# First three outputs behind five layer norms: un-normed sums, corrected afterwards

## The reference

```
def layer_norm(x, g, b):
    mu = mean(x); xc = x - mu; var = mean(xc * xc)
    return xc * rsqrt(var + 1e-5) * g + b

for layer in (0, 1):
    x = layer_norm(ALPHA * x + 0.5 * ff(x, ...), g[layer, 0], b[layer, 0])
    mix = rglru_block(x) if layer == 0 else dilated_attention(x, k, v)
    x = layer_norm(ALPHA * x + mix, g[layer, 1], b[layer, 1])
    x = layer_norm(ALPHA * x + 0.5 * ff(x, ...), g[layer, 2], b[layer, 2])
    if layer == 0: k, v = x @ kv_w
```

## Time and profile before

| | us |
|---|---|
| median of three runs | 1878.16 |
| lowest, highest | 1875.6, 1890.77 |
| span of the profiled execution | 1878.1 |
| PE busy in it | 1823.2 (97%) |
| DVE, ACT, POOL busy | 1263.5, 1160.7, 408.0 |

### The profile page before, as it was taken

How to read it: one execution, slowest core, us unless ns; L and a number is a source line. 1 busy time by engine, 2 the same in 40 slices (tenths; PEclk the granted TensorE clock), 3 DMA queues, 4 the chain that set the end, 5 groups by cost and what they waited for, 6 DMA issues and landing times.

```text
span 1878.1 us, 32925 instructions
## 1 busy us (share of the span) xinstructions
PE 1823.2 (97%) x11312; PEld 1606.1 (86%) x11312; DVE 1263.5 (67%) x1912; ACT 1160.7 (62%) x1894; POOL 408.0 (22%) x442
## 2 busy tenths in 40 slices
PE   7999999999899999999999999999999999999998
PEld 6879888898688888888898988889888888778887
DVE  5877676774766857666668867666566566666665
ACT  4465574643555746488638868844588454759863
POOL 1103330230441402011122032212021120541212
PEclk9999999999899999999999999999999999999999
DMA  6515356557433555555643546663555636126562
GB/s 232 174 57 179 102 194 187 185 184 197 133 107 111 191 188 185 186 186 185 215 162 135 181 134 202 202 209 116 196 184 197 204 128 207 51 79 201 186 222 74
DMA packets 86764, 312.11 MB, mean 166 GB/s; under 512 B 10368, under 2 KB 15616, under 8 KB 86400
## 3 DMA queue, kind: packets, MB, share of 16 engines
q1 hardware_dynamic: 86368, 309.01, 50.6%
q10 hardware_dynamic: 288, 1.64, 0.3%
HBM read 309.56 MB, written 1.05 MB: 165 GB/s over the span
## 4 chain that ended last, share of the span: by engine, by line
PE 89%; DVE 6%; ACT 2%; issue 2%; POOL 1%; DMA 0%; POOLq 0%; SPq 0%; ACTq 0%; DVEq 0%
PE pt L505 42%; PE pt L506 21%; PE pt L499 5%; PE pt L500 5%; PE pt L501 5%; DVE w_lo L1852 1%; PE pt L619 1%; PE pt L623 1%; PE pt L621 1%; PE pt L1149 1%; PE pt L934 1%; DVE in_both L1880 1%; ACT w_hi L1260 1%; PE pt L636 0%; PE pt L1052 0%
## 5 line engine op out<-in xcount | busy, mean ns | idle before, releaser
L1852 DVE TENSOR_TENSOR w_lo<-raw,w_hi 128x1024 fp32r<-128x1024 f32 (+2 forms) x548 | 706.0, 1289 | 290.6 <-ACT w_hi L1260 282.6
L1260 ACT ACTIVATE w_hi<-raw 128x1024 fp32r<-128x1024 f32 (+2 forms) x548 | 598.7, 1095 | 403.6 <-PE pt L506 227.4
L505 PE MATMUL pt<-in_both,w_hi 128*128 128x512 f32 x2103 | 740.4, 397 | 0.5 <-DVE in_both L2434 0.5
L506 PE MATMUL pt<-in_both,w_lo 128*128 128x256 f32 x2103 | 588.5, 280 | 0.0
L505 PEld LDWEIGHTS pt<-in_both,w_hi 128*128 128x128 f32 x2103 | 395.4, 188 | 97.0 <-DVE w_lo L1852 1.1
L505 PE MATMUL pt<-act_both,w_hi 128*128 128x512 f32 x1309 | 463.0, 398 | 0.0
L506 PEld LDWEIGHTS pt<-in_both,w_lo 128*128 128x128 f32 x2103 | 397.2, 189 | 0.1
L506 PE MATMUL pt<-act_both,w_lo 128*128 128x256 f32 x1309 | 366.3, 280 | 0.0
L505 PEld LDWEIGHTS pt<-act_both,w_hi 128*128 128x128 f32 x1309 | 245.7, 188 | 60.5 <-issue 1.7
L506 PEld LDWEIGHTS pt<-act_both,w_lo 128*128 128x128 f32 x1309 | 246.9, 189 | 0.2
L2606 POOL TENSOR_TENSOR act_both<-scr,act_both 128x256 f32 x88 | 99.8, 1134 | 494.7 <-ACT act_both L1739 494.7
(11 more groups left out here) (328 smaller groups left out, 2308.3 us busy)
## 6 DMA issues: line engine op xcount, KB each, us to landing
raw<-in_fi SPq DMA_DIRECT2D x176, 512.0 KB, 3.6
raw<-in_ff SPq DMA_DIRECT2D x128, 512.0 KB, 3.5
raw<-in_fo SPq DMA_DIRECT2D x64, 704.0 KB, 4.1
raw<-in_dq SPq DMA_DIRECT2D x24, 512.0 KB, 3.7
raw<-in_mq SPq DMA_DIRECT2D x16, 512.0 KB, 3.7
raw<-in_mo SPq DMA_DIRECT2D x16, 512.0 KB, 4.0
raw<-in_rg_u SPq DMA_DIRECT2D x10, 512.0 KB, 3.4
raw<-in_rg_y SPq DMA_DIRECT2D x10, 512.0 KB, 3.6
```

The source lines that it names most:

```text
L505: nc.tensor.matmul(pt[:, b, :], lhs_hi, both.rearrange("p t s -> p (t s)"), start=start, stop=False)
L506: return nc.tensor.matmul(pt[:, b, 0:S], lhs_lo, both[:, 0, :], start=False, stop=stop)
L1260: nc.scalar.activation(w_hi[:, u.slot(), w], raw[:, u.slot(), w], ACT.Copy).then_inc(hi_split, 1)
L1852: v.tensor_tensor(w_lo[:, u.slot(), w], raw[:, u.slot(), w], w_hi[:, u.slot(), w].bitcast(F32), ALU.subtract).then_inc(lo_split, 1)
```

## The change

At norms 0 to 4 the first three outputs of the next projection no longer wait for the normed input. With g and b the gain and bias, m the rest of the mean and r the inverse root, W(g * (y - m) * r + b) = (W(g*y) - m * Wg) * r + Wb. So ACT and DVE write z = g*y in high and low parts over parts of act_both that are free (`z_high`, `z_low`), with g and b as two more columns (258 in all), and PE makes the three outputs from z (`from_normed_sums`). Between its second and third chunk PE also makes the sums of the norm, now with a square matrix of ones and 256 columns, so that mean and variance stand on all partitions; root and inverse are taken on 128 x 256. DVE then corrects the three outputs (`z_columns`, `z_open`, `z_scale`). All other outputs use the normed input as before, the fourth being the first that waits for it. For each stage behind a norm the corrected outputs get steps of their own (`first_outputs` for swiglu, `first_conv0` and a convolution from SBUF for rg, linked blocks for kv_k and dq). POOL takes off the mean from all eight chunks instead of five. Norm 5 is as before (`last_norm`).

The diff, cut to its core:

```diff
+Z_WIDE = 3
...
+            def from_normed_sums(name, n):
+                z = z_both(n)
+                pe.wait_ge(acc_free, LN_ACC[n] + DC - 1)
+                for k in range(DC):
+                    pe.wait_ge(z_ready, DC * n + k + 1)
+                    w = slice(k * P, k * P + P)
+                    for j in range(Z_WIDE):
+                        u = UNIT0[name] + j
+                        if k == 0:
+                            pe.wait_ge(lo_split, u + 1)
+                        o = pt[:, j, 0:S + 2]
+                        mm = three(o, w_hi[:, u % RING, w], w_lo[:, u % RING, w], z[:, k, 0, :], z[:, k, 1, :],
+                                   k == 0, k == DC - 1)
+                        if k == DC - 1:
+                            mm.then_inc(unit_used, 1)
+                    if k == 1:
+                        pe.wait_ge(rest_part, 3 * n + 3)
+                        nc.tensor.matmul(pt[:, 6, 0:S], ones, rest_sum, start=True, stop=True).then_inc(rest_ready, 1)
+                        pe.wait_ge(sq_sum, 6 * (n + 1))
+                        nc.tensor.matmul(pt[:, 4, 0:S], ones, spare[:, 0, :], start=True, stop=False)
+                        pe.wait_ge(lnsq_ready, DC * (n + 1))
+                        nc.tensor.matmul(pt[:, 4, 0:S], ones, spare[:, DC - 1, :], start=False, stop=True
+                                         ).then_inc(var_ready, 1)
...
-                if upm == 1 and wait_src:
+                if normed is not None:
+                    from_normed_sums(name, normed)
+                    done = Z_WIDE
...
-                                if k + j == 0 and wait_src:
+                                if k + j == (0 if normed is None else Z_WIDE) and wait_src:
...
+                        if n == Z_WIDE:
+                            pe.wait_ge(in_ready, IN0["ln0"] + k + 1)
...
+                    if m.base == DC - 1 and n in (0, 2, 3):
+                        z_gains_hi(n)
+                        for k in range(DC - 1):
+                            z_high(n, k)
                     if m.base > FIRST_MEAN:
                         act.wait_ge(acc_free, LN_ACC[n] + m.base + 1)
                         square(m.base)
+                    if m.base == FIRST_MEAN + 1 and n in (1, 4):
+                        z_gains_hi(n)
+                        for k in range(FIRST_MEAN + 2):
+                            z_high(n, k)
+                    if m.base == DC - 2 and n in (1, 4):
+                        z_high(n, DC - 2)
...
+            def z_gains_hi(n):
+                act.wait_ge(unit_used, LN_LAST[n] if n in (0, 2, 3) else LN_LAST[n] - DC + 2)
+                nc.scalar.activation(z_both(n)[:, :, 0, S:S + 2], z_gains(n), ACT.Copy).then_inc(z_gains_high, 1)
+            def z_high(n, k):
+                nc.scalar.activation(z_both(n)[:, k, 0, 0:S], y[:, k, :], ACT.Copy, scale=gain("lng", n * DC + k)
+                                     ).then_inc(z_hi_ready, 1)
+            def shift(n, out, k):
+                return nc.scalar.activation(out[:, k, :], y[:, k, :], ACT.Identity, bias=gain("lnb", n * DC + k))
+            def layer_norm(n):
+                split(Pos(LN_LAST[n] + RING))
+                z_high(n, DC - 1)
+                act.wait_ge(rest_ready, n + 1)
+                nc.scalar.activation(spread_wide, pt[:, 6, 0:S], ACT.Square, scale=1.0 / D).then_inc(rest_squared, 1)
+                nc.scalar.activation(mean_wide, pt[:, 6, 0:S], ACT.Copy, scale=1.0 / D).then_inc(rest_copied, 1)
+                act.wait_ge(var_done, n + 1)
+                nc.scalar.activation(spread_wide, spread_wide, ACT.Sqrt, bias=lneps).then_inc(ln_root, 1)
+                for k in range(DC):
+                    act.wait_ge(ln_scaled, DC * n + k + 1)
+                    shift(n, in_hi, k).then_inc(in_hi_ready, 1)
+                for k in range(DC):
+                    shift(n, x, k).then_inc(ln_out, 1)
...
+                def first_outputs():
+                    u0 = UNIT0[f"fi{l}{f}"]
+                    s0 = Z_SCALED0[f"fi{l}{f}"]
+                    split(Pos(u0 + RING))
+                    act.wait_ge(z_scaled, s0 + 1)
+                    nc.scalar.activation(act_a[0], act_b[0], ACT.Silu, bias=z_cols[:, 1:2]).then_inc(silu_ready, 1)
+                    split(Pos(u0 + 1 + RING))
+                    act.wait_ge(unit_used, u0 + Z_WIDE)
+                    after(Pos(1))
+                    split(Pos(u0 + 2 + RING))
+                    act.wait_ge(z_scaled, s0 + 2)
+                    nc.scalar.activation(act_a[1], act_b[1], ACT.Silu, bias=z_cols[:, 5:6]).then_inc(silu_ready, 1)
+                    act.wait_ge(unit_used, u0 + 4)
+                    half(Pos(3))
+                    split(Pos(u0 + 3 + RING))
+                    after(Pos(3))
+                if n in (2, 5):
+                    first_outputs()
+                    units(f"fi{l}{f}", before=half, after=after, begun=4)
+                else:
...
+            def first_conv0(j):
+                act.wait_ge(z_scaled, j + 1)
+                nc.scalar.activation(z_first[j], z_first[j], ACT.Identity, bias=z_cols[:, 2 * j + 1:2 * j + 2]
+                                     ).then_inc(u_made, 1)
+                act.wait_ge(u_made, j + 1)
+                nc.scalar.activation(big[:, j, :], z_first[j], ACT.Identity, bias=gain("cb", j),
+                                     scale=gain("cw", 3 * RC + j)).then_inc(conv0, 1)
+            for j in range(Z_WIDE):
+                split(Pos(UNIT0["rg"] + j + RING))
+                first_conv0(j)
+                if j == 0:
+                    act.wait_ge(unit_used, UNIT0["rg"] + Z_WIDE)
+                else:
+                    conv_hi(j - 1)
+            nc.scalar.activation(warm, eps, ACT.Tanh)
             for n, (kind, i) in enumerate(RG_ORDER):
...
+            def z_low(n, k):
+                dve.wait_ge(z_hi_ready, DC * n + k + 1)
+                z = z_both(n)
+                v.scalar_tensor_tensor(out=z[:, k, 1, 0:S], in0=y[:, k, :], scalar=gain("lng", n * DC + k),
+                                       in1=z[:, k, 0, 0:S].bitcast(F32), op0=ALU.mult, op1=ALU.subtract
+                                       ).then_inc(z_ready, 1)
+            def z_ahead(n):
+                def go():
+                    dve.wait_ge(z_gains_high, n + 1)
+                    z = z_both(n)
+                    v.tensor_tensor(z[:, :, 1, S:S + 2], z_gains(n), z[:, :, 0, S:S + 2].bitcast(F32), ALU.subtract)
+                    for k in range(3):
+                        z_low(n, k)
+                return go
+            def scaled(n, k):
+                dve.wait_ge(recentred, DC * n + k + 1)
+                v.scalar_tensor_tensor(out=y[:, k, :], in0=y[:, k, :], scalar=gain("lng", n * DC + k),
+                                       in1=rstd_all, op0=ALU.mult, op1=ALU.mult).then_inc(ln_scaled, 1)
+            def layer_norm(n):
+                for k in range(3, DC - 1):
+                    z_low(n, k)
+                split(Pos(LN_LAST[n] + RING))
+                z_low(n, DC - 1)
+                dve.wait_ge(var_ready, n + 1)
+                dve.wait_ge(rest_squared, n + 1)
+                v.scalar_tensor_tensor(out=spread_wide, in0=pt[:, 4, 0:S], scalar=1.0 / D, in1=spread_wide,
+                                       op0=ALU.mult, op1=ALU.subtract).then_inc(var_done, 1)
+                dve.wait_ge(ln_root, n + 1)
+                v.reciprocal(rstd_all, spread_wide).then_inc(ln_inverse, 1)
+                dve.wait_ge(ln_inverse, n + 1)
+                for k in range(DC + 2):
+                    if k < DC:
+                        scaled(n, k)
+                    if k >= 2:
+                        dve.wait_ge(in_hi_ready, IN0[f"ln{n}"] + k - 1)
+                        v.scalar_tensor_tensor(out=in_lo[:, k - 2, :], in0=y[:, k - 2, :],
+                                               scalar=gain("lnb", n * DC + k - 2), in1=in_hi[:, k - 2, :].bitcast(F32),
+                                               op0=ALU.add, op1=ALU.subtract).then_inc(in_ready, 1)
+            def z_columns(name):
+                dve.wait_ge(unit_used, UNIT0[name] + Z_WIDE)
+                link(v.tensor_copy(z_cols.rearrange("p (j t) -> p j t", t=2), pt[:, 0:Z_WIDE, S:S + 2]))
+            def z_open(name, j, dest):
+                v.scalar_tensor_tensor(out=dest, in0=mean_wide, scalar=z_cols[:, 2 * j:2 * j + 1], in1=pt[:, j, 0:S],
+                                       op0=ALU.mult, op1=ALU.subtract).then_inc(acc_free, 1)
+            def z_scale(name, j, dest, factor):
+                dve.wait_ge(acc_free, ACC0[name] + j + 1)
+                return v.scalar_tensor_tensor(out=dest, in0=dest, scalar=-factor, in1=rstd_all,
+                                              op0=ALU.mult, op1=ALU.mult)
...
+                def first_outputs():
+                    u0 = UNIT0[name]
+                    z_columns(name)
+                    z_open(name, 0, act_b[0])
```

(48 more changed lines are left out.)

205 lines of the change are left out of this document (108 added, 97 removed).

## The result

The changed kernel takes **1904.86 us** (median of four runs, 1900.63 to 1905.85) against 1880.6 us for the kernel before on the same chip (four runs): ratio 1.0114, 95% interval 1.0091 to 1.0138. It is 1.1% slower. The profiled execution has a span of 1904.0 us, 25.9 us more than the earlier trace rows.

The account below looks back on a forecast made before the run. PE was taken as the bound, holding 89% of the chain. 1878.1 us, plus 10.3 for lags at five norms, 2.5 for one clock fall and 1 for DVE beside POOL, gave 1892 us; range 1867 to 1904.

Parts of the forecast that it names:

- The likeliest case: Whole kernel: the prediction's own forecast, 1892 us, 0.7% slower, within 1884 to 1897; chance 0.50.
- DVE beside POOL: At each norm, DVE work slowed beside POOL: 0.2 us per norm, 1 us in all.
- the clock: PE's granted clock falling around output five: 0 to 8 us together, one fall of 2.5 us taken.
- The wait at the norm goes: PE at norm 1: 5.6 us lost before; now three outputs end at +9.8 rather than +14.1.
- The x writes stand ahead of the fifth split, and output five comes later than before: ACT at norm 1: x writes end at +16.05, then the split; PE idles 4.4 us, starting output five at +18.35, before +17.1.
- The chain to output five: Norm 1: reciprocal from +4.9, last low part of the normed input at +13.45, output five at +18.35.
- The rival in which DVE and POOL take turns: Scalings beside POOL's subtractions: 3 us per norm, 13 in place of 1 in all, 1904 us; chance 0.08.
- That rival (0.15): Granted clock falls at every norm: 8 us in place of 2.5, 1897.5 us; chance 0.15.
- Norm 0: Recurrent block (rg), where ACT and DVE set the pace: conv(3) at +27.9, second gate at +32.9, lag +5.1 us.
- Norms 1, 2, 4: Lags of +2.65, -0.7 and +2.9 us, from late weight splits and steps on ACT and DVE.
- Norm 3: Query projection (dq): output eight ends at +30.3, before +30.0, a lag of +0.3 us.
- Nothing is given back behind output eight: Stages behind the norms: lags stay whole; said at norm 0, where nothing behind has less to do.

## Where the prediction was right and where it was wrong, point by point

The likeliest case, 1892 us, was 12.9 us too low, and the time lies 0.9 us above the upper end of 1904. Part of that is the base: the forecast started from 1878.1 us, and the kernel before took 1880.6 beside the changed one. Taken as a slowdown, 13.9 us were forecast and 24.3 measured, a ratio of 1.007 against 1.011, and the upper end of the range, 1.014, holds. The direction and the mechanism were right, the size was too small: two terms of the sum, DVE beside POOL and the clock, were mis-sized. The chance of "slower by over 1%" was put at 0.20; with an interval of 0.9 to 1.4% the result does not quite decide that.

*The wait at the norm goes.* Right: matmuls of 258 columns follow the last output at once at four norms, 0.69 us late at norm 4; the three outputs end at +10.2 (said +9.8).

*The x writes stand ahead of the fifth split, and output five comes later than before.* Right, and the heart of it: gap 4.13 us (said 4.4), released by DVE's w_lo behind ACT's x writes at all five norms. The run with two splits moved ahead cuts it to 1.11 us.

*The chain to output five.* Here a term was mis-sized, **DVE beside POOL, taken as 0.2 us per norm**. It is 2.4: 1.45 at three scalings and 0.95 at two of the low parts of z, which I had not looked at for it at all. So the reciprocal started at +5.9 instead of +4.9, the last in_lo ended at +15.6 instead of +13.45, output five started at +20.4 instead of +18.35. Over the five norms this makes about 8 of the 15.6 us by which the measured lags (25.8) exceed the reckoned 10.3. I took the price from L2434 in the earlier trace rows, which has two SBUF operands as well. It obeys the same 0.28 us behind POOL's end and lost less only because a scaling that read PSUM stood ahead of it each time, so that it started later in POOL's subtraction; three such instructions in a row each meet nearly a whole one. The rows for that stood in the trace of before. The rival in which DVE and POOL take turns had the right mechanism and the right place; it deserved more than 0.08, since the scaling's operand had been moved from PSUM to SBUF by this very change. But its price was 3 us per norm where 1.45 was measured at the scalings, and it had neither the low parts nor the falls of the clock in it: that its 1904 us is the measured time is luck.

*The clock.* I reckoned one fall in the likeliest case; there were five, and a sixth in do. That rival (0.15) came true beside the other. By the run with the gap filled it cost 1.4 us at norm 2, 1.5 at norm 3, 0.8 at norm 4 and nothing at norm 1, where unit six was late anyway; with the 1.5 in do (by the traces alone, and not in every execution) that is 5.2 us, where 2.5 were charged. Against it I had held that the wait was half a microsecond shorter than before; it was 3.4 to 4.1 us without a single matmul, while before small matmuls of the column sums stood in it. Whether that is the difference, no run shows.

*Norm 0.* Lag 6.6 us (said 5.1), conv(3) at +29.7 (said +27.9), second gate at +34.7 (said +32.9): the order was followed rightly, everything 1.8 us later by the same term. The run with norm 0 restored gives it back whole.

*Norms 1, 2, 4.* Output eight ended at +33.1, +33.2, +34.1 (said +31.15, +29.95 for what kv_v waits for, +31.8): the late chain 1.9, 1.8 and 1.5, and at norms 2 and 4 the clock.

*Norm 3.* The lag of 6.6 us (said 0.3) was the largest miss: output eight ended at +33.0 instead of +30.3 (chain 1.2, clock 1.5); the slower pace of dq took 1.1 us more, the clock in do 1.5. These two were in no case of mine. Nor was the last 1 us between dq and norm 4: do begins 0.3 us later (idle 2.46 instead of 2.18), and at its end PE waits 0.69 us for DVE's first low part of norm 4, which ends at 1697.62:

```profile
1696.43 0.59 PE L626 MATMUL pt<-scr,con 128*128 128x256 f32 x2
1697.72 0.36 PE L524 MATMUL pt<-act_both,w_hi 128*128 128x258 f32 x1 [0.69 <-issue]
```

The prediction had the late high parts of norm 4 and moved all of that norm by 0.6 for them, but counted from its zero; the wait stands ahead of it.

*Nothing is given back behind output eight.* Right: where pace and clock were equal, as behind norm 1, the lag at output eight (4.6) is that of the whole stretch (4.56).

## What to carry to other kernels

A wait that is taken away on the bound engine only helps if the helpers' lists behind it are in the order in which that engine now wants things: here the same edit cost 1.1%, and with two splits moved ahead of copies that nobody waited for, and the root in PSUM, no longer anything. When an operand moves from PSUM to SBUF, count every instruction of DVE with two SBUF operands that will stand beside POOL, and charge each one the rest of the POOL instruction on which it falls, which depends on what stands between them. Apply such a change norm by norm: where the helpers set the pace (rg) it lost 6.6 us, and still 3.4 with both edits that helped.
